# Two-layer hybrid backbone step on one Trainium2 core: the first expert turn's gate and up products taken half by half, and half of its weight buffers refilled before the token rows of the next turns are loaded

## The reference, cut to what matters

```python
g_logits = (u @ p['moe_w_group'][l] + p['moe_b_group'][l]).astype(f32)
...
hg = jnp.einsum('bld,edf->blef', u, p['moe_w_gate'][l])
hu = jnp.einsum('bld,edf->blef', u, p['moe_w_up'][l])
h = jax.nn.silu(hg) * hu * gates.astype(u.dtype)[..., None]
return jnp.einsum('blef,efd->bld', h, p['moe_w_down'][l])
```

## Time and profile before

| | |
|---|---|
| median of three runs | 1223.74 us (1223.24 to 1226.55) |
| the profiled execution, its own time | 1224.85 us |
| its span in the trace | 1223.0 us |
| mean granted clock of TensorE | 0.966 of full |
| PE busy | 1114.9 us, 91% |
| DVE, ACT, POOL busy | 32%, 19%, 12% |
| moved by DMA | 338.24 MB, 277 GB/s in the mean |

### The profile page before, as it was taken

One profiled execution on the slowest core, in us unless ns is written; L12 is line 12 of the kernel. 1 busy time (PEld: TensorE's weight loads), 2 busy tenths in 40 slices (PEclk: granted clock), 3 DMA queues, 4 the chain that ended last, 5 costly groups with the idle time before them and its releaser, 6 DMA issues.

```text
span 1223.0 us, 23538 instructions
## 1 busy us (share of the span) xinstructions
PE 1114.9 (91%) x10201; PEld 622.1 (51%) x10201; DVE 389.9 (32%) x1023; ACT 233.9 (19%) x501; POOL 140.8 (12%) x163
## 2 busy tenths in 40 slices
PE   5899999899989959988889999999998995998986
PEld 3443445555575535545455555545666553555543
DVE  3201331574251300111233633587624230101104
ACT  2002201321231111101053232321012111111112
POOL 1043100022120000000010000042232000000001
PEclk9999999999989989999999999999998998999998
DMA  9998755359559998999996202002395999899994
GB/s 385 398 304 288 312 206 209 145 174 406 200 233 336 405 386 331 371 395 417 416 324 209 73 16 69 1 1 69 153 360 218 367 407 383 324 374 398 406 419 176
DMA packets 73018, 338.24 MB, mean 277 GB/s; under 512 B 6740, under 2 KB 16243, under 8 KB 58128
## 3 DMA queue, kind: packets, MB, share of 16 engines
q1 hardware_dynamic: 60760, 299.14, 63.2%
q0 software_dynamic: 10864, 36.42, 8.6%
q10 hardware_dynamic: 1288, 1.14, 0.3%
HBM read 314.24 MB, written 22.44 MB: 275 GB/s over the span
## 4 chain that ended last, share of the span: by engine, by line
PE 68%; DMA 18%; DVE 7%; issue 2%; ACT 2%; SPq 1%; POOL 1%; ACTq 0%; DVEq 0%; POOLq 0%
PE ps L2359 16%; DMA ring<-in_moe_w_up 12%; PE ps L1987 11%; PE ps L2562 10%; PE ps L2065 8%; PE ps L2383 7%; PE ps L2622 3%; DMA ring<-in_rec_w_in 3%; PE ps L2008 2%; PE ps L2292 2%; PE ps L2592 1%; PE ps L2342 1%; PE ps L2369 1%; PE ps L1980 1%; ACT work L1183 1%
## 5 line engine op out<-in xcount | busy, mean ns | idle before, releaser
L2359 PE MATMUL ps<-ring,work 128*32 128x256 f32 x4736 | 295.8, 394 | 53.4 <-DMA ring<-in_moe_w_up 49.3
L2359 PEld LDWEIGHTS ps<-ring,work 128*32 128x32 f32 x4736 | 150.4, 113 | 152.4 <-issue 66.3
L2562 PE MATMUL ps<-uT,ring 128*128 128x386 f32 x384 | 128.8, 488 | 0.9 <-issue 0.9
L2383 PE MATMUL ps<-ring,work 128*32 128x256 f32 x1728 | 103.0, 380 | 2.1 <-DVE work L1814 2.1
L2562 PEld LDWEIGHTS ps<-uT,ring 128*128 128x128 f32 x384 | 71.7, 190 | 49.6 <-issue 2.4
L1814 DVE COPY work<-ps 128x128 f32<-128x128 f32 x74 | 21.5, 291 | 235.4 <-PE ps L2369 234.3
L2065 PE MATMUL ps<-uT,ring 128*128 128x384 f32 x256 | 89.2, 505 | 3.0 <-DMA ring<-in_rec_w_in 1.9
L1195 ACT ACTIVATE work<-ps 128x128 f32<-128x128 f32 x74 | 20.5, 277 | 337.0 <-PE ps L2359 337.0
L1987 PE MATMUL ps<-ring,uT 128*128 128x512 f32 x192 | 84.1, 595 | 0.0
L2383 PEld LDWEIGHTS ps<-ring,work 128*32 128x32 f32 x1728 | 55.8, 110 | 39.8 <-DVE work L1814 3.0
L1810 DVE TENSOR_TENSOR work<-ps,work 128x128 f32<-128x128 f32 x74 | 21.6, 292 | 155.6 <-ACT work L1195 155.6
(11 more groups left out here) (371 smaller groups left out, 1194.9 us busy)
## 6 DMA issues: line engine op xcount, KB each, us to landing
ring<-in_moe_w_gate SPq DMA_DIRECT2D x32, 2048.0 KB, 12.8
ring<-in_moe_w_up SPq DMA_DIRECT2D x32, 2048.0 KB, 18.0
ring<-in_ada_w SPq DMA_DIRECT2D x24, 2048.0 KB, 11.3
ring<-in_moe_w_down SPq DMA_DIRECT2D x22, 2048.0 KB, 24.1
uT<-in_moe_w_down SPq DMA_DIRECT2D x10, 1536.0 KB, 16.4
ring<-in_rec_w_in SPq DMA_DIRECT2D x6, 2048.0 KB, 23.5
ring<-in_hy_w_in SPq DMA_DIRECT2D x6, 2048.0 KB, 13.4
y_rows<-work SPq DMA_DIRECT2D x64, 96.0 KB, 12.7
```

The lines of the kernel that those rows point to most:

```text
L2359: ins = pe.matmul(bank(key)[32 * q:32 * q + 32, 0:2 * P].rearrange("p (a n) -> p a n", a=2), xg[:, u, k, 32 * i:32 * i + 32], ring[:, 3 * ...
L2383: ins = pe.matmul(bank(key)[32 * q:32 * q + 32, 0:256], hT[:, (FIRST[p] + i) % 2, 32 * k:32 * k + 32], w[:, q * 256:(q + 1) * 256], start= ...
L2562: ins = pe.matmul(bank(key)[:, 0:T + 2], w[:, k, (m % 4) * P:(m % 4 + 1) * P], uH[:, k, :], start=(k == 0), stop=(k == DC - 1))
```

## The change

Turn 0 takes half 0 of all three tiles first and then half 1 of all three. The three tiles stay open in banks 0, 1 and 5. The last matmul of half 0 signals `half_spent`, and on that SP loads the first four features of turn 2's gate and up matrices (two DMAs of 1 MB each) into the part of slots 0 and 1 that is no longer read. Only then does it wait for the rows of turns 1 and 2, and then loads the other four features (two more DMAs of 1 MB). Since slots 0 and 1 are loaded in one more piece in each layer, the counts that PE waits for are raised by one load. ACT waits before the third tile's silu until the first tile's result has been used, since two buffers serve three tiles. Three semaphores at the start of the program are merged into one, `rec_small_cleared`.

```diff
+                if p == 0:
+                    for i, b in enumerate((0, 1, 5)):
+                        claim((l, p, "GU", i), b)
                 for i in range(TILES[p]):
                     par = (FIRST[p] + i) % 2
-                    claim((l, p, "GU", i), par)
+                    if p:
+                        claim((l, p, "GU", i), par)
...
-                slot_uses[s] += {2: 6, 5: 5}.get(s, NE // 2)
+                slot_uses[s] += {0: NE // 2 + 1, 1: NE // 2 + 1, 2: 6, 5: 5}.get(s, NE // 2)
...
+                def load_rows(kind, e, ks, at):
+
+                    n = ks.stop - ks.start
+                    sp.dma_start(ring[:, kind, at * DE:(at + n) * DE].rearrange("p (k n) -> p k n", k=n),
+                                 moe_src(l, kind, e)[:, ks, :]).then_inc(S(f"slot{kind}_loaded"), 16)
...
-                    full(sp, (l, p, "GU", TILES[p] - 1))
                     if p == 0:
+                        sp.wait_ge(S("half_spent"), l + 1)
+                        for kind in range(2):
+                            load_rows(kind, e, slice(0, 4), 0)
                         sp.wait_ge(S("rows1_loaded"), 16 * (l * (NE // 2) + 1))
                         sp.wait_ge(S("rows0_loaded"), 16 * (l * (NE // 2 - 1) + 1))
-                    load_part(0, e, u)
-                    load_part(1, e, u)
+                        full(sp, (l, p, "GU", TILES[p] - 1))
+                        for kind in range(2):
+                            load_rows(kind, e, slice(4, 8), 4)
+                    else:
+                        full(sp, (l, p, "GU", TILES[p] - 1))
+                        load_part(0, e, u)
+                        load_part(1, e, u)
...
                 for i in range(TILES[0]):
+                    if i >= 2:
+                        evacuated(act, (l, 0, "GU", i - 2))
                     silu(0, i)
...
-                                pe.wait_ge(S(f"slot{n}_loaded"), 16 * (base[n] + 1 + p // 2))
+                                pe.wait_ge(S(f"slot{n}_loaded"), 16 * (base[n] + 1 + p // 2 + (1 if u == 0 and p else 0)))
...
                     if half == 1:
                         done(ins, key)
+                    elif p == 0 and i == TILES[0] - 1:
+                        ins.then_inc(S("half_spent"), 1)
...
-                both_halves(0, 0)
-                both_halves(0, 1)
+                for half in range(2):
+                    for i in range(TILES[0]):
+                        gate_up(0, i, half)
                 hidden_t(0, 0)
-                both_halves(0, 2)
                 hidden_t(0, 1)
                 down(0, 0)
                 down(0, 1)
```

More of the change, by code:

```diff
@@ L790, in clear @@
                 pool.memset(ap, 0.0).then_inc(S(name), 1)
-            clear(wg, "wg_cleared")
+            clear(wg, "rec_small_cleared")
             clear(zeros[:], "zeros_cleared")
-            clear(gkw, "gkw_cleared")
+            clear(gkw, "rec_small_cleared")
             clear(g36, "g36_cleared")
-            clear(mcol, "mcol_cleared")
+            clear(mcol, "rec_small_cleared")
             pool.memset(vb[:, :, :, DV:DV + 1], 1.0).then_inc(S("vb_ones"), 1)
             pool.wait_ge(S("slot2_loaded"), 32)
-            pool.wait_ge(S("wg_cleared"), 1)
+            pool.wait_ge(S("rec_small_cleared"), 1)
             w_in = A["rec_w_in"][0].rearrange("(k p) n -> p k n", p=P)
@@ L807, in _ @@
                                w_in[:, :, base + 8 * d + 4 * typ:base + 8 * d + 4 * typ + 4]).then_inc(S("wg_loaded"), 16)
-            pool.wait_ge(S("gkw_cleared"), 1)
+            pool.wait_ge(S("rec_small_cleared"), 2)
             for d in range(2):
                 pool.dma_start(gkw[16 * d:16 * d + 16, 256 * d:256 * d + 256], A["gla_gk_w"][0, d]).then_inc(S("rec_small_loaded"), 16)
-            pool.wait_ge(S("mcol_cleared"), 1)
+            pool.wait_ge(S("rec_small_cleared"), 3)
             for d in range(2):
@@ L1389, in _ @@
             full(v, "gk")
-            v.wait_ge(S("gkw_cleared"), 1)
+            v.wait_ge(S("rec_small_cleared"), 2)
             free(v.tensor_copy(gkT, bank("gk")[0:32, 0:T]), "gk")
```

## The result

The changed kernel takes 1236.40 us, the median of four runs (1233.83 to 1240.97); the kernel before, measured beside it, 1223.49 us (1219.07 to 1226.55, four runs). The ratio is 1.0121 with a 95% interval of 1.0095 to 1.0146: **slower, by 12.9 us**. Two later measurements of the changed kernel don't repeat this verdict: on four other chips the kernel before was itself about 11 us slower, and on the two of them where the changed kernel was run, the change made no difference.

What follows compares the result with a forecast made beforehand. Up to turn 6 the weight stream on q1 was taken to bound the kernel. Later rows less slack gave +0.1 and +1.2 us, one clock fall +1.7: +3.0 us in all, 1226.7 us forecast, range 1220.0 to 1231.0.

Steps and rivals of the forecast that it cites:

- rows later: Turn 1's start: rows of turns 1 and 2 come 2.7 and 3.3 us later in the two layers; bounds none to 4.9.
- the slack of the stream: Weight stream at turn 5's pair: an earlier start can win at most 2.6 and 2.1 us in the two layers.
- the clock: PE at turn 1: idle 2.6 and 3 us, clock falls to the lower level in one of two layers, +1.7 us.
- The scatter's pace: Token-row scatter beside the half loads: pieces alternate, 146 GB/s, its rest takes 4.6 and 5.4 us, not 1.6 and 1.8.
- Rival D: Weights go first: scatter stands still for 2.1 MB, rows 4.9 us late, both clocks fall; +8.5 us, 1232.2; chance 0.05.
- The half loads: SP in turn 0: first half loads issued at about 360.2 and 937.2 us, while the scatter still runs.
- Goes into the wait of 13.3 us and costs nothing.: PE ahead of turn 6: its own delay of 2.7 to 5 us is absorbed by the wait for weights there.
- rival A: PE at turn 1's first products: the clock falls in both layers; +4.7 us, 1228.4, slower; chance 0.25.
- The other edits: Turn 0's new product order, third tile's silu wait, merged semaphores and two more DMA issues a layer: cost nothing.

Runs made afterwards that it cites:

- e1: Changed kernel with the early half loads moved behind the rows of turns 1 and 2, new order kept: 1222.90 us against 1223.73, ratio 0.9990.
- h2: The kernel before, unchanged, run once more for its profile on a fifth chip: 1234.24 us, ratio 0.9993 to the same kernel's runs beside it.
- e2: Changed kernel with the half loads also waiting until the scatter has landed, so only the row loads meet them: 1240.86 us, ratio 1.0138 to the kernel before.
- f1: The changed kernel, unaltered, measured again on a third chip against the kernel before: 1233.82 us, ratio 0.9996.
- e7: Changed kernel with the early loads as four of 512 KB (4 KB pieces) in place of two of 1 MB: 1234.83 us, ratio 1.0090 to the kernel before.
- h1: Kernel before with POOL issuing the scatter only behind turn 0's second tile, on a fifth chip: 1247.77 us, ratio 1.0158.

## Why the prediction was wrong

The form of the sum was right: rows later, less the slack of the stream, plus the clock. Three of its terms were mis-sized, all to the same side.

- **The scatter's pace (the main error).** Predicted: the queues alternate at once, 146 GB/s for the scatter, rows 2.7 and 3.3 us later. Measured: X 7.2 and 7.3 us later. Of it the scatter takes 6.4 and 6.1 us more (18.2 and 18.4 in place of 11.7 and 12.3). The rest is how this execution began (the scatter's first issue stands 1.6 and 1.3 us later against turn 0 than in the execution before, as in e1; in both kernels it stands either 1.2 to 1.4 us ahead of turn 0 or 0.2 us behind it, in h2 one of each, so this part is chance) less 0.8 and 0.1 us of quicker row loads. The earlier trace rows show two queues that were both well under way; what the prediction needed was how waiting work of the software queue fares when q1 fills, and no row of before showed that. Its own upper bound, 4.9 us, was passed too: it counted the 2.1 MB at 428 GB/s, but from 359 to 369 us the two queues together moved 3.50 MB, 350 GB/s, at which 2.1 MB take 6.0 us.
- **Rival D** came nearest, with rows 4.9 us late and 1232.2 us. Its mechanism, all weights first, is not what the change's queues show: the standstill lasts two microseconds, then pieces alternate. So its nearness is in part luck. It was given 0.05. The Trainium skill ("DMA: Bandwidth & Descriptors", section "Queues, rings and completion order") has each engine drain a packet of some 9 to 17 descriptors of one ring before it turns to the next. (A packet in the profile's lines is one piece.) In the standstill the trace agrees with it in kind, 98 packets of q1 against 11 of the scatter in two microseconds, that is six of q1's on each of the 16 engines and less than one of the scatter's; three microseconds later it doesn't, 60 against 66.
- **The half loads were earlier than predicted**, 357.97 us in place of 360.2, so more of the scatter was still to come. Half 0 of three tiles is 96 records, 5.3 us behind a start that in this execution was 352.53. Against the scatter's first issue the half loads stand at 5.3 us in both layers, where the prediction's times make 7.2 and 6.9 (it also counted turn 0 from 354.64 us, 0.24 us late).
- **The slack of the stream.** Predicted 2.6 and 2.1 us, at turn 5's pair. Measured 1.5 and 1.1 us, and at another place: in the changed kernel q1 runs dry just before `step(1)` (394.93 us, silent for 1.2 us), and from there to turn 6 it needs 70.3 us, whatever was loaded before. All runs in which it ran dry there have 70.0 to 71.3 us. The landing time of turn 5's pair, from which I took the slack, went from 14.4 to 13.3 us only.
- **"Goes into the wait of 13.3 us and costs nothing."** Wrong as an account of cover: PE's wait ahead of turn 6 stayed 12.74 us while PE was 7.7 us later. PE's release of turn 1's slots starts the stream that the wait is for (`step(1)` waits for turn 1's last product), so the wait moves along with PE. Whatever makes turn 1 late is paid in full, less that 1 to 1.5 us.
- **The clock.** Predicted one fall of 1.7 us; both layers fell (rival A, 0.25), and `step(1)` stands 2.0 and 3.4 us further behind X. In the second layer the next group is slow too, 2.82 us in place of 1.93. With the rows 7 us late no other outcome was seen in any run. The Trainium skill ("TensorE: Matmul & The Clock Gate", section "Why this matters for your kernels") asks for gaps under about 3 us. The waits for turn 1's rows of 3.3 us and more, up to 7.7 us, were all followed by the lower level, as it says; other waits don't follow it either way, since the lower level came behind 2.60 us and did not come behind a wait for weights of 3.32 us in e2.
- **The other edits at nothing:** right, e1.

## What to carry to other kernels

A load moved into an "idle" stretch of a hardware queue is not free if the software queue is working then and its result has no cover: the other queue's waiting work can stand still first, and share only afterwards. Before counting a long wait as cover, ask what starts the transfer it waits for; if it is a release of the same engine, the wait moves with the lateness and covers nothing. And measure on more than one chip and day where products and a dense transfer overlap: the same change lost 1.2% where it was first measured and nothing on two other chips, where PE was late in any case.

## What the runs showed of the hardware

- **Loads in a software queue that hadn't started were held up when q1 filled:** first packets 3.9 us behind the issue (e2; 3.4 to 3.8 us in f1) in place of 1.3, and the scatter in the change at 11 packets in the 2 us from 361 us, after 151 in the 2 us from 358. Why is open; e7 says that the size of the other queue's pieces is a part of it.
- **A scatter of 4 KB pieces can hold up PE.** On four of the chips that were used the kernel before takes 1234 to 1236 us in place of 1223.5. Gaps of 0.8 us among turn 0's products, and slow records hidden in a row of 70 (5.6 us where 70 take 3.9), make X 4.4 to 5.1 us later in each layer, some 9.5 of these 11 us (h2). They move with the scatter (h1). Each chip was measured in one session, and each kernel there profiled once, so whether the gaps belong to the chip or to the time of measuring isn't shown, and their cause stays open.
- **The stream takes 70.0 to 72.2 us from `step(1)` to turn 6** in all profiles of the table, on all chips, with or without gaps, and however late turn 1 was.
